# Weight halves made by DVE instead of POOL in blocks two and three, with a later bias table and reordered LRU and SSD

## What is computed

```python
xbc = silu(causal_dwconv(u_xbc, conv_w, conv_b))          # 12 tiles of 128 channels, 4 taps
seg = a_cs[..., :, None] - a_cs[..., None, :]             # SSD: 16 heads, chunks of 64
decay = exp(where(causal, seg, -inf))
y_diag = einsum("bgcls,bgecls,bcsgep->bclgep", cb, decay, xdt)

xc = causal_dwconv(u_x, conv_w, conv_b)                   # RG-LRU: 8 tiles of channels
log_a = -LRU_C * r * softplus(-lam); a = exp(log_a)
mult = sqrt(-expm1(2.0 * log_a))
bx = mult * i * xc                                        # then h = a * h_before + bx, and h * gate

h = causal_dwconv(h @ w_up, conv_w, conv_b)               # FFN, 6144 columns, 3 taps, gelu gate, then down
```

## Time and profile before

| what | value |
|---|---|
| median of 3 runs | 2131.33 us (2128.96 to 2131.94) |
| the profiled execution | 2139.45 us |
| its span in the trace | 2137.7 us |
| granted TensorE clock, mean share of full speed | 0.857 |
| busy: PE, DVE, ACT, POOL | 1575.8, 758.0, 579.0, 614.3 us |
| bytes moved | 570.06 MB, 267 GB/s over the span |

### The profile page before, as it was taken

One profiled execution on the slowest core, in us unless ns is written; L12 is line 12 of the kernel. 1 busy time (PEld: TensorE's weight loads), 2 busy tenths in 40 slices (PEclk: granted clock), 3 DMA queues, 4 the chain that ended last, 5 costly groups with the idle time before them and its releaser, 6 DMA issues.

```text
span 2137.7 us, 25344 instructions
## 1 busy us (share of the span) xinstructions
PE 1575.8 (74%) x10341; PEld 1066.2 (50%) x10341; DVE 758.0 (35%) x989; ACT 579.0 (27%) x973; POOL 614.3 (29%) x252
## 2 busy tenths in 40 slices
PE   4979786566566765666565689687789787889897
PEld 2758641111111211111111279676779777888797
DVE  3325420000000000000000189797839884176343
ACT  4324430000000000000000234645544344445453
POOL 1144300000000000000000058344648465655473
PEclk8989888877878687887878879899889897998898
DMA  9455559999999999999999825223325332433330
GB/s 395 141 200 229 236 236 428 428 429 428 429 429 428 429 429 428 430 428 428 430 428 429 381 99 186 90 80 118 119 79 197 118 124 112 166 140 113 115 119 20
DMA packets 48292, 570.06 MB, mean 267 GB/s; under 512 B 4576, under 2 KB 10720, under 8 KB 11744
## 3 DMA queue, kind: packets, MB, share of 16 engines
q1 hardware_dynamic: 40992, 556.81, 63.4%
q10 hardware_dynamic: 7232, 12.29, 2.1%
HBM read 564.89 MB, written 4.19 MB: 266 GB/s over the span
## 4 chain that ended last, share of the span: by engine, by line
DMA 37%; PE 29%; DVE 25%; ACT 3%; issue 2%; DVEq 1%; another core or an unknown queue 1%; ACTq 0%; POOL 0%; SPq 0%
PE bank L1373 29%; DMA ring<-in_w_down 12%; DMA ring<-in_w_up 12%; DMA ring<-in_w_gate 12%; DVE work L810 4%; DVE work L157 4%; DVE work L806 3%; DVE work L155 1%; ACT work L1689 1%; DMA ring<-in_dense 1%; DVE work L728 1%; DMA ring<-in_w_ada 1%; DVE rstd L1927 1%; DVE work L1931 1%; ACT weights_high_rounded L1689 1%
## 5 line engine op out<-in xcount | busy, mean ns | idle before, releaser
L1354 POOL TENSOR_TENSOR ring_rounded<-ring,weights_high_rounded 128x1024 fp32r<-128x1024 f32 x244 | 609.0, 2508 | 1475.1 <-ACT weights_high_rounded L1689 1474.3
L1373 PE MATMUL bank<-ring,work 128*32 128x512 f32 x3008 | 483.8, 776 | 309.7 <-DMA ring<-in_w_up 125.3
L1689 ACT ACTIVATE work<-bank 128x256 f32<-128x256 f32 (+3 forms) x312 | 137.5, 447 | 1188.5 <-PE bank L1373 833.4
L1373 PEld LDWEIGHTS bank<-ring,work 128*32 128x32 f32 x3008 | 93.1, 126 | 665.5 <-DMA ring<-in_w_up 207.6
L1689 ACT ACTIVATE weights_high_rounded<-ring 128x1024 fp32r<-128x1024 f32 x244 | 256.0, 1053 | 33.1 <-PE bank L1373 22.3
L1373 PE MATMUL bank<-h_high_rounded,weights_high_rounded 128*128 128x256 f32 x1296 | 208.6, 302 | 54.5 <-ACT weights_high_rounded L1689 35.9
L2140 DVE TENSOR_TENSOR work<-work,bank 128x512 f32<-128x512 f32 x16 | 16.5, 1030 | 592.3 <-PE bank L1373 592.3
L1373 PEld LDWEIGHTS bank<-h_high_rounded,weights_high_rounded 128*128 128x128 f32 x1296 | 178.7, 200 | 74.2 <-issue 39.3
L1373 PE MATMUL bank<-h_normed_rounded,weights_high_rounded 128*128 128x256 f32 x1296 | 187.1, 290 | 0.0
L1373 PE MATMUL bank<-h_high_rounded,ring_rounded 128*128 128x256 f32 x1296 | 182.8, 285 | 2.6 <-POOL ring_rounded L1354 2.5
L1373 PE MATMUL bank<-work_rounded,weights_high_rounded 128*128 128x256 f32 x1088 | 162.6, 301 | 29.1 <-ACT work_rounded L1689 20.2
(11 more groups left out here) (230 smaller groups left out, 1363.4 us busy)
## 6 DMA issues: line engine op xcount, KB each, us to landing
ring<-in_w_down SPq DMA_DIRECT2D x64, 2048.0 KB, 16.2
ring<-in_w_gate SPq DMA_DIRECT2D x63, 2048.0 KB, 16.2
ring<-in_w_up SPq DMA_DIRECT2D x61, 2048.0 KB, 16.4
ring<-in_dense SPq DMA_DIRECT2D x60, 2048.0 KB, 7.7
ring<-in_w_ada SPq DMA_DIRECT2D x12, 2048.0 KB, 20.4
work<-in_w_up SPq DMA_DIRECT2D x3, 1024.0 KB, 13.2
bias_diagonals<-work ACTq DMA_DIRECT2D x2, 1532.0 KB
ring<-in_dense SPq DMA_DIRECT2D x2, 1024.0 KB, 18.8
```

Of the source, the lines that this page charges most:

```text
L1354: nc.gpsimd.tensor_tensor(as_r(w), w, w_high[:, buffer, :], ALU.subtract).then_inc(s.w_low, 1)
L1373: return nc.tensor.matmul(o, lhsT, rhs, start=start, stop=stop)
L1689: return nc.scalar.activation(o, i, f, **kw)
```

## The change

Three things are changed.

1. **The low halves of blocks two and three go from POOL to DVE.** POOL's loop over 208 units is gone. A helper `weight_low(unit)` waits on DVE for `w_high` and does the same subtraction; calls of it are written by hand between DVE's other steps: one after each convolution, one in each turn of the head loop, two after each pair of the FFN's convolutions, the rest between the steps of the projections, the merge, the norms and block three.

2. **The LRU and the SSD are reordered.** The masked decay rows are made by ACT (an Identity with a scale by partition; three buffers instead of two) and no longer by DVE. Before, the LRU's decay a came from a tanh by way of a reciprocal; now ACT writes the tanh into XC and makes a with an Exp (8 more ACTIVATEs of 128x256 and one more table load); `lru_input` with its RECIPROCAL is gone, as is the multiplication by -4 (the Sqrt takes a scale of -1). The product of i and xc is made ahead of the SSD's transposes, and `masked(h+1)` runs one head ahead.

3. **The bias table is made later.** ACT loads its constants (`BUCKETS`, in other tiles) after the first unit of the LRU projection, PE makes the rows after unit 2 of the SSM projection, ACT copies them after unit 3 and issues the same two stores there. ACT's wait before unit 12 of block one and PE's before block 4 of `w_ada` are gone. New waits for `toep_stored`: DVE's before the FFN's first convolution, since the tiles in which the table lies are written there, and ACT's before it loads the biases in block three.

```diff
-            with pool.Fori(0, D2_BLOCKS // RING) as r:
-                for j in range(RING * UNITS):
-                    pool.wait_ge(s.w_high, r * (RING * UNITS) + (D1_UNITS + j + 1))
-                    low(D2_BLOCK0 + j // UNITS, j % UNITS, (D1_UNITS + j) % HIGHS)
+            def weight_low(unit, turn=None):
+                at, buffer = D1_UNITS + unit, (D1_UNITS + unit) % HIGHS
+                dve.wait_ge(s.w_high, at + 1 if turn is None else turn * ROUND + (at + 1))
+                w = unit_weights(d2_block(unit), unit % UNITS)
+                v.tensor_tensor(as_r(w), w, w_high[:, buffer, :], ALU.subtract).then_inc(s.w_low, 1)
...
+            weights_low(0, 2)
             norm_invert(5)
             norm_to(5, H, X, par("mix_pre"), HH)
+            weights_low(2, AHEAD2)
...
             for n in range(KT):
                 last = conv(n, n, 13 + n, "lru_conv_w", "lru_conv_b")
-            last.then_inc(s.xc_ready, 1)
+                if n == KT - 1:
+                    last.then_inc(s.xc_ready, 1)
+                weight_low(13 + n + AHEAD2)
+            weights_low(21 + AHEAD2, 32 + AHEAD2)
...
             for h in range(SSM_H):
-                dve.wait_ge(s.seg_exp, h + 1)
-                v.tensor_tensor(SEG[h % 3], SEG[h % 3], CBM[:, h // 8, :], ALU.mult).then_inc(s.m_ready, 1)
+                if h + 1 < SSM_H:
+                    masked(h + 1)
                 if h + 2 < SSM_H:
                     segments(h + 2)
-                if h + 3 < SSM_H:
-                    mask_decay(h + 3)
-                if h % 2 == 0:
-                    lru_input(h // 2)
-                else:
+                if 38 + h < IN2:
+                    weight_low(38 + h + AHEAD2)
+                if h % 2:
                     lru_scan(h // 2).then_inc(s.act_full, 1)
...
+            dve.wait_ge(s.toep_stored, 32)
             with dve.Fori(0, 1) as r:
                 for j in range(8):
                     conv_pair(r, 0, j)
+                    for unit in (2 * j, 2 * j + 1):
+                        weight_low(L_UP + unit + AHEAD2, r)
...
             for k in range(KT):
-                last = fn(TH[:, k, :], TH[:, k, :], ACT.Tanh, scale=LAMC[:, k:k + 1])
+                fn(XC[:, k, :], TH[:, k, :], ACT.Tanh, scale=LAMC[:, k:k + 1])
+            for k in range(KT):
+                last = fn(TH[:, k, :], TH[:, k, :], ACT.Exp, scale=LAMT[:, k:k + 1])
...
             for n in range(8):
                 copy2(L_SSM + n, PA[:, n, :])
+                if n == 3:
+                    for kind in range(2):
+                        act.wait_ge(s.toep_mm, kind + 1)
+                        fn(TW[0:AH, kind, 0:TOEP], B[4 + kind][0:AH, 0:TOEP], ACT.Copy).then_inc(s.toep_sb, 1)
+                    act.wait_ge(s.toep_sb, 2)
+                    for kind in range(2):
+                        act.dma_start(d["toep"][kind * AH:(kind + 1) * AH, :, 0:TOEP],
+                                      spread(TW[0:AH, kind, 0:TOEP], 1, P)).then_inc(s.toep_stored, 16)
...
             for pu, (unit, a, t) in enumerate(DENSE1):
-                if unit == 12:
-                    act.wait_ge(s.toep_stored, 32)
```

More of the change, by code:

```diff
@@ L286, in program @@
         MIX_HIGH = tiles3(0, 8)
-        STARTERS = tiles(16, 7)[:, 0:START_COLS]
+        BUCKET_COLS = START_AT["ahead"][0]
+        STARTERS = tiles(16, 7)[:, BUCKET_COLS:START_COLS]
         KQ = tiles3(16, 8)
@@ L510, in soft, with mask_decay @@
                 return fn(t, t, ACT.Ln, bias=1.0)
+            def mask_decay(h):
+                if h >= 3:
+                    act.wait_ge(s.bc_mm, h - 2)
+                fn(LMASK[h % 3], LCUM, ACT.Identity, scale=con("head_rows")[:, h:h + 1]).then_inc(s.lmask_ready, 1)
             squares_of_x(s.x_ready, KT)
@@ L667, in vector_block2 @@
             link(v.tensor_tensor(LAMC, LAMC, LAMT, ALU.add))
+            v.tensor_scalar(LAMT, LAMC, -8.0, None, ALU.mult)
             v.tensor_scalar(LAMC, LAMC, -4.0, None, ALU.mult).then_inc(s.lam_ready, 1)
+            weights_low(32 + AHEAD2, 35 + AHEAD2)
+            for k in range(KT):
+                i = tiles(I_OF[k], 1)
+                dve.wait_ge(s.ri_sig, k + 1)
+                last = v.tensor_tensor(i, i, XC[:, k, :], ALU.mult)
+            last.then_inc(s.ixc_ready, 1)
+            weight_low(35 + AHEAD2)
             dve.wait_ge(s.ssd_tr, 1)
@@ L677, in vector_block2 @@
             dve.wait_ge(s.cs_ready, 1)
-            for h in range(2):
-                v.tensor_scalar(LMASK[:, h, :], LCUM, con("head_rows")[:, h:h + 1], None, ALU.mult).then_inc(s.lmask_ready, 1)
             for g in range(2):
@@ L787, in vector_block2 @@
             add_normed(6, MO2, par("mix_post"))
+            weight_low(L_UP - 1 + AHEAD2)
             norm_invert(7)
@@ L818, in vector_block2 @@
                     conv_pair(r, 1, j)
+                    for unit in (2 * j, 2 * j + 1):
+                        weight_low(L_UP + ROUND + unit + AHEAD2, r)
                     for k in (2 * j - 4, 2 * j - 3):
@@ L1975, in _, with weights_low @@
                                    op1=ALU.subtract).then_inc(s.decay_ready, 1)
+            def weight_low(unit, turn=None):
[3 more added lines that the diff above has]
+                v.tensor_tensor(as_r(w), w, w_high[:, buffer, :], ALU.subtract).then_inc(s.w_low, 1)
+            def weights_low(first, end):
+                for unit in range(first, end):
+                    weight_low(unit)
             def modulation(r):
```

119 lines of the change are left out of this document (71 added, 48 removed).

## The result

The changed kernel takes 2029.42 us (median of 4 runs, 2028.09 to 2031.13) against 2130.68 us before (4 runs, 2128.96 to 2131.94): a ratio of 0.9526 with a 95% interval of 0.9509 to 0.9542, 101 us less. The forecast was 2031. Its profiled execution took 2029.78 us, with a span of 2028.0, so it lies on its median, which that of before did not (2139.45). The difference of the two traces is therefore 109.7 us, 8 more than the medians differ, and the one trace of before does not tell in which stages its 8 us lie.

The account below looks back on a forecast made before the run. PE waits for the experts' weights early; DVE, held by POOL's low halves, bounds long stretches of blocks two and three. Gains summing to 100 us took the profiled 2139.45 to 2039, less 8 for the median: 2031, 8-in-10 range 2005 to 2066.

Parts of the forecast that it names:

- Early stretch: Before the experts: PE's gaps from the two stores and a late load go; 20 us gained, bounds 12 to 24.
- rival 3: The early gain does not carry or is half as large, a load being late: about 2047 us, 12%.
- Into block two: At block two's start: POOL's four low halves no longer hold DVE's norm; some 7 us gained.
- In-projection and head loop: PE's 15.79 us wait goes, net 11.6 us gained; the loop becomes bound by PE, 15.8 us gained.
- Projections and merge: PE's waits for the merge's roundings shrink, ACT's standing queue just covered: 3.8 us gained, bounds -6 to 8.
- Rival 5: Low halves in the wrong place of DVE's fixed order reach PE late, twenty places at 1.2 us: 2055 us, 12%.
- FFN up: FFN's up units: DVE stays the bound, 155 us instead of 185, less a stall of 2 for the stores: 28 gained.
- The rest: Norms 6 and 8 and block three: fewer PE waits for DVE; 14 us gained, bounds 5 to 18.
- the slower one: DVE's steps stay long for another cause than POOL, so the added low halves cost time: 2190 us, 4%.
- the even swap: DVE was held by each low half only as long as it now takes there; some 20 us gained: 2091, 4%.
- the sixth: Better: with fewer gaps PE's clock stays at 1.00, where it was 0.90 in the FFN's window: 2012 us, 9%.
- The rule that I had set against the sum: The Trainium skill: GPSIMD and DVE share a read port, so offloading between them might not help; the move would give nothing.

Follow-up runs that it names:

- part three alone: The kernel before with only the bias table made later, low halves still on POOL and LRU and SSD as before: 2111.84 us, ratio 0.9908.
- The run without part two: The changed kernel with masked decay rows, reciprocals and the old order back on DVE in the head loop: 2033.59 us, ratio 0.9544.
- the run with POOL's needless work: The changed kernel plus 44 POOL subtractions of 128x1024 during the FFN, on data nobody reads: 2114.25 us, ratio 0.9904.

## Why the prediction was right, and where it was not

The time came to 2029.42 for 2031, and the direction and the main cause hold: POOL's low halves held DVE, and went cheaper on DVE itself. Several terms of the sum were mis-sized, and they are named below. Step by step, with the two traces' stages:

- **The price of a low half**: 1.22 us taken, 1220 ns measured.
- **Early stretch**: 20 us taken. PE's unit of 149.38 us starts at 126.16 in the changed kernel, 23.2 earlier, and at the experts' end it is 27.4. In the three kernels of the table with the stores in block one the mark at the experts' end lies between 1215.29 and 1219.70, in the other four between 1190.68 and 1192.77, so the last 4 us of the 27.4 are within their spread. The gain carries; rival 3 falls with the run of part three alone.
- **Into block two**: 7 taken, 27.73 to 19.40 is 8.3.
- **In-projection and head loop**: 11.6 + 15.8 = 27.4 taken; from the last in-projection unit to the LRU projection it was 129.25 and is 101.53, 27.7. The wait of 15.79 went. Up to y(0) it is 12.7 for 11.6, and from there 15.0 for 15.8, so both sizes held. What was off is the account of the loop: I credited all of it to the 44 us of work that part two takes off DVE. The run without part two shows that 6.2 of the 15.0 come without it, and that of its 8.8 it gives 5.4 back ahead of y(0), where ACT's new work stands (I had counted 4.2, and no table load). All in all part two brings 3.5 us of this stage. I had read DVE's busy time as work, when part of it was hold.
- **Projections and merge**: I took 3.8, on the step that ACT's 9.57 us in its queue are "just covered" by PE's four units in stock, and 1.3 for norm 6. Measured 80.41 to 76.61, so 3.8 for the merge and the norms; the LRU projection ahead of them took 1.7 more (27.76 to 29.45), so 2.1 for all of it. That it came near was luck, two errors against each other: the stores cost 11.7 us there and the freed merge and norm gave 15.5 (80.41 to 64.87). I had counted PE's stock but not what is queued on DVE behind a step that waits for ACT. Rival 5 named this kind of place, and the largest one was here.
- **FFN up**: 28 taken, 35.1 measured (215.60 to 180.48). DVE's 24 pairs with their gatings and splits took 185.1 us in the trace of before (1600.10 to 1785.16), as I had, and take 151.1 now (1533.43 to 1684.55), for 155. The step that was mis-sized is a pair of convolutions at 6.0 us in all three rounds. In round one a pair takes 5.6 us, since its steps follow each other without the pauses of 0.18 and 0.28 us, and there PE bounds and DVE waits:

```profile
1539.02 0.42 DVE L845 TENSOR_SCALAR work<-work,params 128x256 f32<-128x256 f32 x1 [0.38 <-ACT work L1746]
1539.47 1.01 DVE L849 SCALAR_TENSOR_TENSOR work<-work,params 128x255 f32<-128x255 f32 x2
1540.51 0.41 DVE L845 TENSOR_SCALAR work<-work,params 128x256 f32<-128x256 f32 x1
1540.96 1.00 DVE L849 SCALAR_TENSOR_TENSOR work<-work,params 128x255 f32<-128x255 f32 x2
1541.88 2.35 DVE L2028 TENSOR_TENSOR ring_rounded<-ring,weights_high_rounded 128x1024 fp32r<-128x1024 f32 x2
1544.60 0.42 DVE L845 TENSOR_SCALAR work<-work,params 128x256 f32<-128x256 f32 x1 [0.37 <-ACT work L1746]
```

  In rounds two and three a pair with its gatings and splits takes 6.0 to 7.3 us, as worked out. DVE is busy 118.73 of 138 us, not near 100%. The wait for the stores never showed: DVE comes to its first convolution 73 us after the issue, as estimated, at 1533.43, and is held by its own input; the stores' last packet ended at 1528.3, 68 us after the issue. So 33.9 us for 30 come from the pairs, the 2 us of the wait fall away, and the start and the tail of the stage give the last 1.2.
- **The rest**: 14 taken; from the second group of FFN down to the end it is 325.93 to 317.39, 8.5. The sum of small gains in block three was too high: its low halves are placed late at some steps (PE waits for one in each layer, 1.75 and 2.21 us). The rest of the 5.5 that are missing stays open.
- **The offset.** I said that the sum made against the profiled time goes over to the medians with the same 8 us. It does not: the changed kernel's profiled run lies on its median. The steps add up to 100.2 and the traces differ by 109.7; the medians differ by 101. The sum was 9.5 us short and the offset 8 us too large; the last digits of the hit are this cancellation, and not precision of the sum.

Of the rivals, the slower one and the even swap are excluded by the run with POOL's needless work, that the stores land late by DVE's rows, and that the change does nothing by POOL's busy time. The condition of the sixth came true, the clock being 1.00 in the FFN's window, but its time of 2012 did not. The rule that I had set against the sum, that a move between POOL and DVE gives nothing, fails here: the move gave 81 us, since POOL held DVE for 1.9 us where DVE needs 1.22.

## What to carry to other kernels

Busy time of an engine may hold time that another engine takes from it: compare the same instruction at places where the other engine runs and where it is idle before counting what its removal frees. An engine with slack is not free to use if its instructions stop a busier one; in this case the engine that does the same work in half the time was the better place, however full it looked. When an engine's queue stands, ask what waits for it on the next engine and what stands behind that; here two large stores held the queue 9 us less when they were issued apart in time.

## What the runs showed of the hardware that I had not expected

- A POOL subtraction of 128x1024 with both inputs in SBUF costs a busy DVE 1.9 us (84.9 us for 44), though its result is used by nobody. The hold does not fall on every DVE instruction. In the timeline of the kernel before, in the head loop:

```profile
1434.18 2.38 POOL L1354 TENSOR_TENSOR ring_rounded<-ring,weights_high_rounded 128x1024 fp32r<-128x1024 f32 x1 [3.10 <-ACT weights_high_rounded L1689]
...
1434.46 0.34 DVE L698 TENSOR_SCALAR work<-bank,small 128x128 f32<-128x128 f32 x1
1434.72 1.99 DVE L728 TENSOR_SCALAR work<-work,consts 128x256 f32<-128x256 f32 x1
```

  L698, whose input is a PSUM bank, starts and ends inside POOL's 2.38 us at its own length; L728, whose input is in SBUF, ends 0.15 us after POOL. Over all 16 heads L698 starts with over 1 us of a POOL instruction left 13 times, and is 0.34 us each time.
- Two stores of 1532 KB in 1532-byte packets issued back to back from ACT hold its queue for 10.81 us; 11 us apart they take 1.29 and 0.68 us. Why the queue stands is not shown.
- The same two stores issued from POOL are out in 2.27 us, but take twice the share of the DMA engines (65.6% against 30.9% of a window of 75 us), and 2 MB loads beside them land after 36.0 us in the median.
